# Two attention blocks spread over their projections: groups of four heads between half chunks, bias and maximum in one instruction per head

## The reference, cut to what matters

```python
# swa: 16 query heads, 4 key/value heads, head width 64, blocks of 128 queries
qkv = h @ w_qkv                                   # 1024 -> 1536
q, k = rmsnorm(q, q_gain), rmsnorm(k, k_gain)     # per head
scores = einsum(q, k) / 8 + alibi                 # a bias that differs per head
scores = where(mask, scores, -inf)
p = softmax(concat([scores, sink]))[..., :-1]
x = x + einsum(p, v) @ w_o                        # 1024 -> 1024
# na: 1024 -> 2304; 8 heads with rotary embedding, a window mask and sinks (2 key/value heads),
# 8 heads with their own keys and a learned bias rpb; softmax; then 1024 -> 1024
```

## Time and profile before

| | |
|---|---|
| time, median of three runs | 1364.94 us (1363.85 to 1365.16) |
| the profiled execution | 1364.45 us, of which the span is 1362.6 us |
| busy in the span | PE 96%, PE weight load 86%, DVE 67%, ACT 51%, POOL 10% |
| `swa`: last q/k/v chunk to first output chunk on PE | 335.3 to 381.1 us |
| `na`: the same | 654.5 to 700.2 us |
[...]

### The profile page before, as it was taken

How to read it: one execution, slowest core, us unless ns; L and a number is a source line. 1 busy time by engine, 2 the same in 40 slices (tenths; PEclk the granted TensorE clock), 3 DMA queues, 4 the chain that set the end, 5 groups by cost and what they waited for, 6 DMA issues and landing times.

```text
span 1362.6 us, 19889 instructions
## 1 busy us (share of the span) xinstructions
PE 1308.6 (96%) x8210; PEld 1168.9 (86%) x8210; DVE 912.6 (67%) x1065; ACT 700.2 (51%) x908; POOL 142.4 (10%) x166
## 2 busy tenths in 40 slices
PE   8999999999899999999898999999999999899997
PEld 7889888888698888898788888879999988888886
DVE  6766655566946655566777665587888775766666
ACT  5445545455645444543654444446877763354442
POOL 0000000004505000000000000000144543000000
PEclk9999999999699999999899999998999999999999
DMA  9555666645139666554124555535444424465551
GB/s 308 189 182 157 199 185 187 190 149 188 30 109 217 213 190 190 180 185 156 63 94 155 194 193 196 191 122 185 125 155 124 155 94 155 155 216 185 186 185 62
DMA packets 221034, 224.61 MB, mean 165 GB/s; under 512 B 7312, under 2 KB 204304, under 8 KB 220816
## 3 DMA queue, kind: packets, MB, share of 16 engines
q1 hardware_dynamic: 217760, 213.94, 49.1%
q10 hardware_dynamic: 2160, 7.31, 1.5%
q0 software_dynamic: 1024, 2.10, 0.9%
HBM read 222.27 MB, written 1.05 MB: 164 GB/s over the span
## 4 chain that ended last, share of the span: by engine, by line
PE 75%; DVE 14%; ACT 4%; issue 3%; DMA 2%; POOL 1%; SPq 0%; DVEq 0%; ACTq 0%
PE ps L480 19%; PE ps L681 17%; PE ps L494 11%; PE ps L482 10%; DVE wlo L1480 4%; PE ps L642 2%; PE ps L462 2%; PE ps L949 2%; ACT whi L1064 2%; PE ps L453 1%; PE ps L452 1%; PE ps L451 1%; DVE ssm_taps L1869 1%; DVE small L1691 1%; DMA raw<-in_ffn_w_gate_up 1%
## 5 line engine op out<-in xcount | busy, mean ns | idle before, releaser
L1480 DVE TENSOR_TENSOR wlo<-raw,whi 128x2048 fp32r<-128x2048 f32 x202 | 461.8, 2292 | 167.1 <-ACT whi L1064 166.9
L480 PE MATMUL ps<-act,whi 128*128 128x512 f32 x1280 | 454.0, 398 | 3.1 <-DVE act L1500 2.4
L1064 ACT ACTIVATE whi<-raw 128x2048 fp32r<-128x2048 f32 x202 | 384.6, 1907 | 55.5 <-PE ps L681 31.3
L482 PE MATMUL ps<-act,wlo 128*128 128x256 f32 x1280 | 359.3, 281 | 0.0
L480 PEld LDWEIGHTS ps<-act,whi 128*128 128x128 f32 x1280 | 240.5, 188 | 63.1 <-DVE wlo L1480 2.6
L482 PEld LDWEIGHTS ps<-act,wlo 128*128 128x128 f32 x1280 | 241.7, 189 | 1.6
L1111 ACT ACTIVATE low_sb<-ps 128x512 f32<-128x512 f32 x88 | 52.5, 596 | 200.3 <-PE ps L482 191.6
L494 PE MATMUL ps<-whi,act 128*128 128x256 f32 x736 | 136.4, 287 | 1.1 <-DVE act L1545 1.1
L494 PEld LDWEIGHTS ps<-whi,act 128*128 128x128 f32 x736 | 116.1, 194 | 2.7 <-DVE act L1545 1.3
L1597 DVE TENSOR_TENSOR sum_sb<-ps,low_sb 128x512 f32<-128x512 f32 x88 | 60.5, 687 | 81.6 <-ACT low_sb L1111 81.6
L681 PE MATMUL ps<-whi,hidhi 128*128 128x512 f32 x368 | 114.3, 392 | 0.0
(11 more groups left out here) (231 smaller groups left out, 2031.5 us busy)
## 6 DMA issues: line engine op xcount, KB each, us to landing
raw<-in_mlp_w SPq DMA_DIRECT2D x128, 512.0 KB, 4.4
raw<-in_ffn_w_gate_up SPq DMA_DIRECT2D x88, 512.0 KB, 5.1
raw<-in_ssm_w_in SPq DMA_DIRECT2D x50, 512.0 KB, 4.7
raw<-in_ffn_w_down SPq DMA_DIRECT2D x44, 512.0 KB, 4.8
raw<-in_conv_w_in SPq DMA_DIRECT2D x24, 512.0 KB, 5.8
raw<-in_attn_w_in SPq DMA_DIRECT2D x18, 512.0 KB, 4.7
raw<-in_ssm_w_out SPq DMA_DIRECT2D x16, 512.0 KB, 4.4
raw<-in_attn_w_qkv SPq DMA_DIRECT2D x12, 512.0 KB, 4.4
```

The source lines that it names most:

```text
L480: e.matmul(ps[:, b + f, :].rearrange("p (a n) -> p a n", a=2), hi[:, k, cols], act[:, :, k, :], start=k == 0, stop=False, skip_group_check ...
L482: last = e.matmul(ps[:, b + f, 0:T], lo[:, k, cols], act[:, 0, k, :], start=False, stop=k == KT - 1, skip_group_check=True)
L1064: e.activation(whi[s][:, :], raw[s][:, :], ACT.Copy).then_inc(*rounded.up(c))
L1480: e.tensor_tensor(wlo[s][:, :], raw[s][:, :], f32(whi[s][:, :]), ALU.subtract).then_inc(*split.up(c))
```

## The change

- Groups are numbered with m fastest (g, m = divmod(n, 2)), so that heads can start as soon as their four queries are there. The order of the q/k/v chunks changes with that (`SWA_ORDER`: keys, values, then queries; `NA_ORDER`).
- PE's list is one sequence written by hand: half chunks (`piece`), transposes, `score`, `turn`, `mix`, and quarters of the first two output chunks (`out_piece`, 12 matmuls). ACT's and DVE's lists are written to match, `hi` and `lo` among them.
- The q/k/v chunks keep banks 0 to 2, so scores have one place (banks 4/5) instead of two, transposed probabilities banks 6/7, and bank 3 serves `mix` and the transposes of queries by turns. `score(n)` waits for `weigh(n-1)` to have read.
- `weigh` reads each head's scores in one fused instruction (`tensor_tensor_reduce`: add bias, scale, running maximum) instead of one addition and one maximum over four heads. Biases are stored divided by the scale.
- `weigh(n+1)` now stands behind `normalise(n)`.

Numbering, and the waits of PE that change with the one place for scores and for `mix`:

```diff
         def swa_group(n):
-            m, g = divmod(n, 4)
+            g, m = divmod(n, MT)
...
+        SWA_ORDER, NA_ORDER = (4, 5, 0, 1, 2, 3), (2, 0, 1, 5, 3, 7, 6, 4, 8)
...
                 def score(n):
...
-                    if n >= 2:
-                        e.wait_ge(*biased(st, n - 2))
+                    if n:
+                        e.wait_ge(*biased(st, n - 1))
...
                 def mix(n):
...
                     e.wait_ge(*probs_copied(st, n))
-                    if n >= 2:
-                        e.wait_ge(*out_lo(st, n - 2))
+                    take(3)
...
+                    free[3] = out_lo(st, n)
```

PE's list in `swa`, from the fifth chunk on:

```diff
+                q_heads(0, 6)
+                piece(4, 0)
+                e.wait_ge(*qk_lo("swa", "k1"))
+                score(0)
+                piece(4, 1)
+                q_heads(1, 3)
+                score(1)
+                turn(0)
+                piece(5, 0)
+                score(2)
+                turn(1)
+                mix(0)
+                piece(5, 1)
+                q_heads(2, 3)
+                score(3)
+                turn(2)
+                mix(1)
+                score(4)
+                out_piece(0, 0)
+                turn(3)
+                mix(2)
+                score(5)
+                out_piece(1, 0)
+                q_heads(3, 3)
+                turn(4)
+                mix(3)
+                score(6)
+                out_piece(0, 1)
+                turn(5)
+                mix(4)
+                score(7)
+                out_piece(1, 1)
+                turn(6)
+                mix(5)
+                out_piece(0, 2)
+                turn(7)
+                mix(6)
+                out_piece(1, 2)
+                mix(7)
+                out_piece(0, 3)
+                out_piece(1, 3)
```

In `na`, PE's list from the transposes on (in the middle it goes on in the same manner), then its end:

```diff
+                heads("q1", 3, cols(2 * P), cols(3 * P))
+                score(0)
+                piece(4, 1)
...
+                heads("k1", 3, cols(1280), cols(1280 + P))
+                score(1)
+                turn(0)
+                piece(5, 0)
+                score(2)
+                turn(1)
+                mix(0)
+                piece(5, 1)
...
+                heads("k2", 3, cols(1280 + 2 * P), cols(1280 + 3 * P))
+                turn(5)
+                mix(4)
+                piece(7, 1)
+                mix(5)
...
+                heads("q3", 3, cols(768 + 2 * P), cols(768 + 3 * P))
+                piece(8, 0)
+                score(6)
+                piece(8, 1)
+                score(7)
+                out_piece(0, 0)
+                out_piece(0, 1)
+                turn(6)
+                out_piece(1, 0)
+                out_piece(1, 1)
+                turn(7)
+                mix(6)
+                out_piece(0, 2)
+                mix(7)
+                out_piece(1, 2)
+                out_piece(0, 3)
+                out_piece(1, 3)
```

ACT's list at the end of `na`:

```diff
+                heads("q3", 3, 2, None, 3)
+                hi(c0 + 10)
+                exps(6)
+                keep(8)
+                exps(7)
+                turn(6)
+                hi(c0 + 11)
+                turn(7)
```

DVE: the fused instruction, then its list in `na`, and the output product's first splits:

```diff
-                    e.scalar_tensor_tensor(out=p4, in0=s4, scalar=SCALE, in1=g["bias"], op0=ALU.mult, op1=ALU.add).then_inc(*biased.up(st, n))
...
-                    e.tensor_reduce(neg, p4, AX, ALU.max).then_inc(*weigh_step.up(st, n))
...
+                    for w in range(4):
+                        last = e.tensor_tensor_reduce(out=p4[:, w, :], in0=s4[:, w, :], in1=g["bias"](w), scale=SCALE, scalar=-3e38,
+                                                      op0=ALU.add, op1=ALU.max, accum_out=neg[:, w:w + 1])
+                    last.then_inc(*biased.up(st, n))
...
+                weigh(1)
+                lo(c0 + 7)
+                normalise(1)
+                weigh(2)
+                rest(0)
+                normalise(2)
...
+                lo(c0 + 9)
+                heads("k2", 3, 0)
...
+                lo(c0 + 10)
+                weigh(6)
+                normalise(6)
+                weigh(7)
+                lo(c0 + 11)
+                normalise(7)
...
-            def project(st, c0, norm):
+            def project(st, c0, norm, split_=0):
                 for n in range(2):
-                    lo(c0 + n + 2)
+                    if n >= split_:
+                        lo(c0 + n + 2)
```

More of the change, by code:

```diff
@@ L407, in sp_program @@
             ffn(FFN1, 1)
-            for n in range(QKV2 // WIDE):
-                columns(NA + n, A["attn_w_in_2"][0], n * WIDE)
+            for n, part_ in enumerate(NA_ORDER):
+                columns(NA + n, A["attn_w_in_2"][0], part_ * WIDE)
             for n in range(4):
@@ L604, in project @@
                     place_of = lambda m, n=n: project_place(n, m)
[L605 to L609, removed]
+                    take(n)
                     e.wait_ge(*split(c))
@@ new lines, in heads @@
+                def heads(key, b, *sources):
+                    if b == 3:
+                        take(3)
+                        free[3] = qk_lo(st, key)
+                    for f, source in enumerate(sources):
+                        for m in range(MT):
+                            last = e.transpose(ps[:, b, f * T + m * P:f * T + (m + 1) * P], source(m), ident)
+                    last.then_inc(*heads_turned.up(st, key))
+                return piece, out_piece, score, turn, mix, heads
@@ L832, in na @@
-                attend("na")
-                free.clear()
-                project("na", NA + 9, 5, lambda p: out_lo("na", 4 + p))
+                piece, out_piece, score, turn, mix, heads = attention("na", NA, NA + 9)
+                cols = lambda c0: lambda m: qkv[:, m, c0:c0 + P]
+                twice = lambda g: lambda m: k_twice[:, m, g * P:(g + 1) * P]
+                first_token_chunks(4, NA)
+                for n in range(2):
+                    free[(NA + n) % SLOTS] = copied("na", n)
@@ L1241, in na @@
-                turn_heads("na", "k0", 4, k_t, 0)
-                turn_heads("na", "q1", 0, q_t, 2)
-                turn_heads("na", "k1", 5, k_t, 2)
-                turn_heads("na", "k2", 6, k_t, 4)
-                turn_heads("na", "q2", 2, q_t, 4)
-                turn_heads("na", "q3", 3, q_t, 6)
-                attend("na")
+                keep, heads, exps, turn, mix = attention("na", c0)
+                for n in range(3):
+                    hi(c0 + n + 2)
+                    keep(n)
@@ new lines, in na @@
+                hi(c0 + 5)
+                heads("k0", 4, 0)
+                heads("q0", 5, 0)
+                keep(3)
+                hi(c0 + 6)
+                heads("q1", 3, 2)
+                exps(0)
+                keep(4)
+                heads("k1", 3, 2)
+                turn(0)
+                exps(1)
+                hi(c0 + 7)
+                turn(1)
+                mix(0)
+                exps(2)
+                keep(5)
+                heads("q2", 3, 0, None, 1)
+                turn(2)
@@ new lines, in na @@
+                mix(1)
+                exps(3)
+                hi(c0 + 8)
+                turn(3)
+                mix(2)
+                exps(4)
+                keep(6)
+                turn(4)
+                mix(3)
+                exps(5)
+                hi(c0 + 9)
+                heads("k2", 3, 0, None, 3)
+                turn(5)
+                mix(4)
+                keep(7)
+                mix(5)
+                heads("q3", 3, 2, None, 3)
+                hi(c0 + 10)
+                exps(6)
@@ new lines, in rope_heads @@
+                    e.tensor_tensor(spread(rot[:, m, half:], [HD, count], [1, half]), near, plus_sin, ALU.mult).then_inc(*rope_step.up(key, m, 0))
+                    e.wait_ge(*rope_step(key, m, 0))
+                    e.tensor_tensor(both, both, cos, ALU.mult).then_inc(*rope_step.up(key, m, 1))
+                for m in range(MT):
+                    v = qkv[:, m, first * HD:]
+                    both, turned_ = spread(v, [HD, count], [1, HD]), spread(rot[:, m, :], [HD, count], [1, HD])
+                    e.wait_ge(*rope_step(key, m, 1))
+                    if key == "k":
+                        last = e.tensor_tensor(spread(k_twice[:, m, :], [2 * HD, 2], [HD, 2], [1, HD]),
+                                               spread(v, [HD, 2], [0, 2], [1, HD]),
+                                               spread(rot[:, m, :], [HD, 2], [0, 2], [1, HD]), ALU.add)
+                    else:
+                        last = e.tensor_tensor(both, both, turned_, ALU.add)
```

527 lines of the change are left out of this document (320 added, 207 removed).

## The result

| | median, us | ratio to before, 95% interval |
|---|---|---|
| before | 1365.05 (1363.85 to 1365.81) | |
| after | 1383.14 (1382.93 to 1383.74) | 1.013 (1.0118 to 1.0143) |

The forecast was 1383, range 1357 to 1397. The sum came out, but not all of its terms did. The profiled execution has a span of 1381.5 us against 1362.6.

What follows compares the result with a forecast made beforehand. Attention was taken to run at DVE's pace, some 4.3 us a group. On the profiled 1364.45 us, `swa` +3.0, `na` +9.8 and half clock +6.0 gave +18.8: 1383, own range 1374 to 1392, whole range 1357 to 1397.

Steps and rivals of the forecast that it cites:

- the knots: `swa` group 1, `na` groups 1 and 7: a split ahead of `normalise` on DVE idles PE 6.9, 5.2, 5.7 us.
- the walk: Step laying PE's, ACT's and DVE's lists side by side with durations, giving times per group: +3.0 us `swa`, +9.8 `na`.
- the waits: PE's new idle time in the attention blocks: 19.1 us `swa`, 19.4 `na`, plus 2.3 and 1.4 waiting for later additions.
- short hand-overs: Small PE waits between steps in the attention blocks, added to the listed waits: 1.4 us in `swa`, 1.1 in `na`.
- the fused group: `weigh` over four heads of 256 keys on DVE: 1.75 us taken, between 1.44 and 2.44, against 2.43 for the old pair.
- the clock: Three PE waits of 5 to 7 us bring three half-clock spells at 2.0 us each: +6.0 us.
- PE's own work: PE's attention work without waiting or half clock: 27.4 us in `swa`, 34.7 in `na`.
- 18.4 and 11.0: Waiting and half clock of PE in before's `swa` and `na` attention, us; together 29.4, all that hiding can give.
- A: Rival: pieces hide the attention, so faster: 1335, or 1344 with half the small waits; needs PE idle under 29 us; chance 0.17.
- B: Rival: every fused head costs 0.61 us (0.48 over 128 keys), +9 us, 1392; chance 0.12.
- C: Rival: clock stays up between waits and the fused instructions cost 1.44 us a group: +9, 1374; chance 0.19.
- D: Rival: no net effect, hand-overs and one long wait cheaper than drawn, within 3 us of before; chance 0.07.

Runs made afterwards that it cites:

- e1: Kernel after with three weight-chunk splits (`lo`) moved behind `weigh(2)` or `normalise(7)` in DVE's list alone: 1367.96 us, ratio 1.0022.
- e6: Kernel after with DVE's list reordered in both attention blocks and ACT's in `swa`, nothing else: 1359.66 us, ratio 0.995.
- e10: Kernel before with only the convolution's output projection taking its PSUM banks one by one instead of all four first: 1362.09 us, ratio 0.9982.
- e7: As e6, but ACT's list stays as in the kernel after, so only DVE's order is changed: 1363.29 us, ratio 0.9988.
- e8: e6 with half of piece 5 in `swa` moved ahead of `turn(0)` on PE: 1357.54 us, ratio 0.9938.
- e9: e8 with `swa`'s fourth query transposes in bank 2 instead of 3 and `out_piece(0, 2)` behind `turn(7)`: 1357.19 us, ratio 0.9928.
- e5: Kernel after with matmuls of zeros (50, 40, 40) in PE's three long waits before held transposes: 1379.79 us, ratio 1.0118.

## Why the prediction came out

**Right: the knots.** The three places, their order on DVE, and ACT as the one who ends DVE's wait are as drawn. PE's waits are 6.2, 4.8 and 4.8 for the 6.9, 5.2 and 5.7 of the walk, DVE's waits before the splits 3.1, 3.9 and 4.9. Mixing 3 waits 1.97 (1.9), quarter (0,2) 2.34 (2.8), the later additions 1.94 and 1.19 (2.3, 1.4). Groups 0 to 7 of `swa` are 7.2 us apart (6.9). e1 shows that these knots are the cause of four fifths of the slowdown.

**Right in direction, too large: the waits.** 42.2 us were forecast in both blocks, 37.0 came. The 2.5 us of "short hand-overs" do not show; the rest, I think, is mostly the fused group at 1.46 us, the lower bound, where the sum took 1.75; no run separates it. The nearest row for an accumulator read, ACT's 0.09, was the wrong neighbour: on DVE the read (0.08) starts with the next head, both at 334.38 in the rows above.

**Too small: the clock.** The step failed in its count and in its size: "three waits of 5 to 7 us should bring three spells" of 2.0, 6.0 us; five spells took 10.6 us of PE time. Waits of 1.9 and 2.3 us brought one each too, while others of 2.0 to 2.7 brought none.

**Missing: PE's own work grows.** Waits and clock, put in place of the old 18.4 and 11.0, give +6.0 for `swa` and +12.2 for `na`, where the milestones show +8.1 and +12.8. Of the 2.7 us left over, 0.6 are the feed-forward stage. The rest is a step that failed: the prediction took PE's own work, 27.4 and 34.7 us, as the same in both orders. Take PE's busy time in each block less what the windows of 4 us give as lost to half clock: it is 77.3 us before and 80.7 after in `swa`, 120.3 and 122.4 in `na`, with the same matmuls. The growth of 3.4 and 2.1 shows in the account only in part, because the 18.4 and 11.0 were too small as well: by the same windows before waits and loses 20.8 and 12.5 us in the two blocks. In `na` one can see it without the clock, since e6 runs the whole block at 1.00 and is busy 122.6 us. The groups of the query/key/value matmuls in `na`, of before and of e6 (busy us, mean ns):

```profile
L494 PE MATMUL ps<-whi,act 128*128 128x256 f32 x288 | 52.8, 286 | 0.0
...
L499 PE MATMUL ps<-whi,act 128*128 128x256 f32 x288 | 55.3, 289 | 0.0
```

It is 52.8 again in e10, in the old order, and 55.3 again in e7, e8 and e9. A half chunk between the groups takes 2.97 to 3.06 us in e6, from its start to that of the next step; the prediction counted 2.88. So cutting the products into pieces costs PE some time of its own, with no wait and no slow clock; what it consists of stays open.

**Missing: the convolution.** -3.4 us in the stage, shown by e10. Its `take` lines stood in the diff, and its wait in the trace of before, but the prediction looked only at the two stages that the change is about.

The account from 18.8: -5.2 (waits), +4.6 (clock), +2.7 (PE's own work and the feed-forward stage, as far as they show), -3.4 (convolution), +1.4 (before 87 us and behind the third milestone, where kernels with the same code there differ by as much: 183.9 in e5, 185.3 in e6 for the next stage) gives 18.9. That the point forecast was right to 0.1 us is luck: errors of 1.4 to 5.2 us cancelled. Its own range, 1374 to 1392, is the better measure of what the argument was worth.

**The rivals.** *A* (pieces hide the attention): its condition, PE idle under 29 us, is not met by after. e6 meets it (13.3 and 4.9 us), and lands at 1359.7, 6.5 below its own before, of which 3.4 are the convolution's and so not the interleaving's. e1 meets it too (24.3 us in all) and is still slower than before: the condition was too weak, since it leaves out the clock and PE's own growth. Its far end, 1335, has come near in no version. *B* (0.61 a head) is excluded by the rows, where a head costs 0.345. That four short rows over 256 columns cost 0.4 us more than one over 1024 did not decide it: the four pairs take 1.46 us and the two instructions over 1024 that they replace take 2.43, one pass over the scores in place of two. *C* had the right price of the fused group (1.44 for 1.46) and the wrong clock. *D* is excluded by the measurement.

## What to carry to other kernels

When work of one engine is spread between pieces of another's, read the lists of all engines at each new joint: a long instruction that itself has to wait (here the scaling of a weight chunk, 3.1 to 4.9 us of wait and 2.29 of work) should not stand in front of the short one that the busiest engine needs next. Here three such places were worth 15.2 us (after less e1). Price every hunk of a diff, also those that look like plumbing: PSUM banks taken one by one were worth 3.4 us of a stage, a fifth of the whole effect. A wait on PE is to be priced with the half clock that may stand behind it: in `na` the two waits of 4.8 us had 5.0 us of half clock behind them, half as much again. And work cut into pieces can cost its engine more than the same work in one stretch, before anything waits: by the account above 3.4 us of PE's busy time in `swa` and 2.1 in `na`.

## What the runs showed of the hardware

- Fused add and maximum with an accumulator on DVE (after): over 256 float32 columns from PSUM a row is 0.41 to 0.42 us and the heads start 0.345 apart (334.04 to 335.07), over 128 columns 0.28 and 0.21 (343.49, 343.70); the read of the accumulator (0.08) has the start of the next head in these rows.
- Waits of 1.9 to 2.3 us on PE between dense stretches were followed by half-clock spells that cost 1.5 to 1.7 us of PE time (384 and 400 us in after, 84 us in before), those of 4.8 to 6.2 us in after (343.63, 654.13, 715.97) by 2.4 to 2.6. But the cost does not follow the length of the wait: one of 2.4 us in e1 (339.52) was followed by 3.0, one of 1.7 in e6 (361.48) by 4.5 (windows 360 to 372), and those of 1.97, 2.26 and 2.69 us in after (367.61, 688.13, 644.09) by none, though the same waits of 1.97 and 2.69 had one of 1.3 each in e5 (windows 364 to 372 and 644 to 652). What tells these apart I can't say from these runs.
- Matmuls of zeros during a wait kept the granted clock at 1.00 through it and directly behind it (e5, windows 344:348, 652:656 and 716:720, where after has 0.50, 0.57 and 0.50); at other waits of that run it fell (0.78 in 364:368, 0.77 in 644:648).
- The 288 `whi,act` matmuls of `na` took PE 52.8 us in chunks one after the other (before, e10) and 55.3 us in half chunks between the groups (e6 to e9), all in windows with a clock of 1.00.
